# A three-block kernel: scale and shift applied to transposed rows at the start, a router in column quarters, and the state-space setup placed under a projection

## The reference, cut to what matters

```python
def first_block(x, c, ...):      # T = 256, D = 1024
    mod = silu(c) @ w_mod + b_mod                  # six vectors of 1024: sh1 sc1 g1 sh2 sc2 g2
    h = layer_norm(x) * (1 + sc1) + sh1            # "first modulation"
    ... = h @ w_in + b_in ...                      # ag, av, v, u, ga, gb
    x = post_norm(alpha * x + g1 * branch)
    h = layer_norm(x) * (1 + sc2) + sh2
    logits = h @ w_router + b_router               # 32 experts
    top 4 of 32 per row, softmax over the four     # "router"
    y = sum over the four of weight * expert(h)    # 32 experts, 12.6 MB of weights each
    return post_norm(alpha * x + g2 * y)
def second_block(...): ...                         # retention and a gated recurrence
def third_block(...):                              # GLA mixer, then an S5 mixer (state space)
    x = x + gla(...)                               # ends in a projection, "go"
    h = rmsnorm(x); u, z = split(h @ s5_w_in)
    # 64 groups x 64 complex states: lam_bar = exp(lam dt), rotate, scan in time, rotate back
    y = gelu(...); y = y * sigmoid(y @ w_glu + b) * silu(z); x = x + y @ w_out
    return rmsnorm(x)
```

## Time and profile before

| what | value |
|---|---|
| time, median of 3 runs | 2265.51 us |
| lowest and highest | 2263.78 and 2267.04 us |
| the profiled execution's own time | 2264.45 us |
| its span, first to last instruction | 2262.6 us |
| PE busy, share of the span | 2132.4 us, 94% |
| DVE, ACT, POOL busy | 782.6, 440.7, 73.0 us |
| mean granted TensorE clock | 0.988 |

### The profile page before, as it was taken

One profiled execution on the slowest core, in us unless ns is written; L12 is line 12 of the kernel. 1 busy time (PEld: TensorE's weight loads), 2 busy tenths in 40 slices (PEclk: granted clock), 3 DMA queues, 4 the chain that ended last, 5 costly groups with the idle time before them and its releaser, 6 DMA issues.

```text
span 2262.6 us, 30802 instructions
## 1 busy us (share of the span) xinstructions
PE 2132.4 (94%) x11644; PEld 1117.4 (49%) x11645; DVE 782.6 (35%) x1897; ACT 440.7 (19%) x886; POOL 73.0 (3%) x95
## 2 busy tenths in 40 slices
PE   6999999989999998999999998999999999998998
PEld 5745564333333333333333335745564446787873
DVE  1794443222222222222222222241212363998100
ACT  1011121101111110111101101031012215897100
POOL 0000000000000000000000000000000000222000
PEclk9999999999999999999999999999999999999999
DMA  9654677989989995998989999435234333232340
GB/s 374 222 187 153 243 281 279 418 337 418 411 351 418 417 417 232 418 416 333 418 344 418 418 418 369 159 126 186 75 126 149 112 119 114 76 113 75 124 159 34
DMA packets 157322, 591.38 MB, mean 261 GB/s; under 512 B 5073, under 2 KB 5137, under 8 KB 124353
## 3 DMA queue, kind: packets, MB, share of 16 engines
q1 hardware_dynamic: 152240, 572.03, 64.6%
q0 software_dynamic: 4384, 16.40, 2.0%
q10 hardware_dynamic: 624, 1.93, 0.2%
HBM read 589.29 MB, written 1.05 MB: 261 GB/s over the span
## 4 chain that ended last, share of the span: by engine, by line
PE 77%; ACT 8%; DMA 6%; DVE 4%; DVEq 2%; issue 1%; ACTq 1%; SPq 0%
PE PS L646 18%; PE PS L977 17%; PE PS L634 10%; PE PS L1000 9%; DMA W<-in_w_gu 5%; PE PS L675 4%; PE PS L661 4%; PE PS L1013 2%; PE PS L924 2%; ACT BIG L1609 1%; PE PS L1261 1%; PE PS L968 1%; DVE BIG L1973 1%; PE PS L941 1%; DVE BIG L1977 1%
## 5 line engine op out<-in xcount | busy, mean ns | idle before, releaser
L977 PE MATMUL PS<-W,BIG 128*64 128x512 f32 x2048 | 448.3, 594 | 6.3 <-DMA W<-in_w_gu 6.2
L646 PE MATMUL PS<-W,BIG 128*128 128x512 f32 x960 | 417.9, 596 | 4.3 <-DVE BIG L2443 2.9
L646 PEld LDWEIGHTS PS<-W,BIG 128*128 128x128 f32 x960 | 182.9, 191 | 231.6 <-issue 226.1
L977 PEld LDWEIGHTS PS<-W,BIG 128*64 128x64 f32 x2048 | 143.5, 137 | 293.3 <-issue 280.0
L1000 PE MATMUL PS<-W,BIG 128*64 128x512 f32 x1024 | 228.2, 598 | 6.9 <-ACT BIG L1423 6.9
L634 PE MATMUL PS<-BIG,W 128*128 128x256 f32 x1024 | 222.2, 379 | 1.5 <-ACT BIG L382 1.5
L634 PEld LDWEIGHTS PS<-BIG,W 128*128 128x128 f32 x1024 | 194.2, 190 | 29.0 <-ACT BIG L382 1.9
L1418 ACT ACTIVATE BIG<-BIG 128x512 f32<-128x512 f32 x32 | 20.2, 630 | 709.6 <-DVE BIG L1971 709.6
L1971 DVE TENSOR_SCALAR BIG<-PS 128x512 f32<-128x512 f32 (+1 forms) x38 | 24.7, 650 | 345.7 <-PE PS L977 321.6
L1000 PEld LDWEIGHTS PS<-W,BIG 128*64 128x64 f32 x1024 | 70.9, 137 | 143.3 <-issue 128.2
L1187 PE MATMUL PS<-BIG,W 128*128 128x256 f32 x512 | 118.7, 386 | 1.5 <-ACT BIG L1578 0.9
(11 more groups left out here) (482 smaller groups left out, 1978.5 us busy)
## 6 DMA issues: line engine op xcount, KB each, us to landing
W<-in_w_gu SPq DMA_DIRECT2D x128, 2048.0 KB, 14.7
W<-in_w_dn SPq DMA_DIRECT2D x64, 2048.0 KB, 15.2
W<-in_w_in SPq DMA_DIRECT2D x24, 2048.0 KB, 18.9
W<-in_w_mod SPq DMA_DIRECT2D x12, 2048.0 KB, 10.9
W<-in_gla_w_in SPq DMA_DIRECT2D x10, 2048.0 KB, 7.9
...
```

The source lines that it names most:

```text
L646: ins = pe.matmul(ps[:, t, :], lhs(i * KT + k)[:, t * P:(t + 1) * P], w[:, k, :], start=i + k == 0, stop=last_chunk and k == KT - 1)
L977: ins = pe.matmul(PS[hh[h], g, :], XET[:, k, :], gu_w(k)[:, g * D + h * CH:g * D + (h + 1) * CH], start=False, stop=k == KT - 1, skip_grou ...
```

## The change

It has three parts and some small ones.

**Head.** SP issues the first six chunks in the order 0, 2, 4, 5, 1, 3 (`HEAD_ORDER`). h1 is now only normed by DVE (one `tensor_scalar` for each row tile) and is transposed at once. `head_rows` makes the first half (512 columns) of sc1 and of sh1; ACT copies both; `head_columns` transposes them, so that each scale and shift value stands on the partition of its column; DVE multiplies and adds the transposed slices 0 to 3 in place. `head_unit` runs the part of ag0 and av0 that needs slices 0 to 3, then the second halves of sc1 and sh1 are made, then the rest of both units runs. No spread of sc1 and sh1 is left.

**Router.** The spread of sc2 stands ahead of the second half of sh2, the spread of sh2 directly behind it; of g2 only the first half is made ahead of the transposes. The logits are 16 matmuls with 128 x 32 weights and 128 columns, in four column quarters of the array (two slices summed in each), copied by DVE, and summed and transposed by two matmuls with `QUARTERS`. The second half of g2, three residual terms and the spread of g2 take the place of `keep_active`. ACT takes the exponentials ahead of the copies of g2, and makes the copies GAIN_Q and GAIN_H that DVE made. The product BDN goes to POOL. All bias sums stand directly ahead of the loop; PE waits for the table of extra blocks inside `extras`.

**State space.** `spread_b`, `rounded`, `turn_b`, `angles` and `trig` of groups 0 and 1 are done while PE runs go1 (with scratch of their own, `ANG` and `RND` in three places); the norm of the first row tile stands between them. u of group 0 is copied and stacked as soon as a quarter of the projection is done. `S5_EARLY` is 13, and in the last but one group the Gelu pass stands ahead of `y_out`.

```diff
-S5_CT, S5_P, S5_I, S5_G, S5_N, S5_EARLY = 16, 64, 16, 64, 128, 12
+S5_CT, S5_P, S5_I, S5_G, S5_N, S5_EARLY = 16, 64, 16, 64, 128, 13
+HEAD_ORDER = (0, 2, 4, 5, 1, 3)
...
+            for n in HEAD_ORDER:
+                mat, r, c = head_chunks[n]
+                sp.dma_start(slot(n), mats[mat][r:r + D, c:c + CH].rearrange("(k p) n -> p k n", p=P)) \
+                    .then_inc(w_landed[slot_no(n)], 16)
...
-                    pool.wait_ge(ev("mod_done"), len(MODS))
+                    pool.wait_ge(unit_free[UNIT["g2"][0] % 2], UNIT["g2"][0] // 2 + 1)
+                    pool.wait_ge(ev("moe_small_landed"), 80)
+                    pool.tensor_tensor(BDN, BDN, MA[0:NE], ALU.mult).then_inc(ev("exp_then_bias"), 1)
...
+                        if between and t + i == 1:
+                            between(t)
...
+            def head_rows(name, i):
+
+                j, at = MODS[name]
+                n = UNIT[name][3] + i
+                o = PS[:, 6 + j, i * P:(i + 1) * P]
...
+                pe.wait_ge(w_landed[slot_no(n)], load_count(n))
+                for k in range(KT):
+                    for q in range(4):
+                        ins = pe.matmul(o[32 * q:32 * q + 32, :], CB[:, k, :], slot(n)[:, k, q * P:(q + 1) * P],
+                                        start=False, stop=k == KT - 1, skip_group_check=True)
+                if name == "sh1":
+                    ins.then_inc(chunk_done, 3 if i else 1)
+
+            def head_columns(i):
+
+                pe.wait_ge(ev("mod_copied"), i + 1)
+                for j in range(2):
+                    ins = pe.transpose(HEAD_PS[:, j, :], MODROW[:, j, i * P:(i + 1) * P], ident)
+                ins.then_inc(ev("mod_done"), 1)
+
+            def head_unit(name, i, ms):
...
+                for m in ms:
+                    for k in range(4 * i, 4 * i + 4):
+                        if name == "ag0" and m == 0:
+                            pe.wait_ge(ev("cond_ready"), k + 2)
+                        ins = pe.matmul(ps[:, m // 2, (m % 2) * T:(m % 2 + 1) * T], slot(c0)[:, k, m * P:(m + 1) * P], hT[:, k, :],
+                                        start=k == 0 and m % 2 == 0, stop=k == KT - 1, skip_group_check=True)
...
+            head_rows("sc1", 0)
             for t in range(TT):
                 pe.wait_ge(ev("rows_ready"), NORMED["h1"] + t + 1)
                 row_to_columns("h1", t, h1[:, t])
...
+            head_rows("sh1", 0)
+            head_columns(0)
+            head_unit("ag0", 0, range(4))
+            head_unit("av0", 0, range(2))
+            head_rows("sc1", 1)
+            head_rows("sh1", 1)
+            head_unit("av0", 0, (2,))
+            head_columns(1)
+            head_unit("av0", 0, (3,))
+            head_unit("ag0", 1, range(4))
+            head_unit("av0", 1, range(4))
...
             mod_rows("sc2")
-            mod_rows("sh2")
+            mod_rows("sh2", (0,))
             mod_spread("sc2")
-            mod_rows("g2")
+            mod_rows("sh2", (1,))
             mod_spread("sh2")
-            mod_spread("g2")
+            mod_rows("g2", (0,))
...
             for t in range(TT):
-                for k in range(KT):
-                    ins = pe.matmul(PS[:, 6, t * NE:(t + 1) * NE], H2T[:, k, t * P:(t + 1) * P], WR[:, k, :],
-                                    start=k == 0, stop=k == KT - 1)
+                pe.wait_ge(tp_copied, TB["h2"] + 2 * t + 2)
+                for i in range(2):
+                    for q in range(4):
+                        k = 4 * i + q
+                        ins = pe.matmul(PS[32 * q:32 * q + 32, 6, t * P:(t + 1) * P], WR[:, k, :], H2T[:, k, t * P:(t + 1) * P],
+                                        start=i == 0, stop=i == 1, skip_group_check=True)
             ins.then_inc(ev("logits_done"), 1)
-
-            keep_active(4, 4)
-            pe.wait_ge(ev("neg_max"), 1)
-            keep_active(4, 2)
-            pe.wait_ge(ev("exp_ready"), 1)
-            keep_active(4, 5)
+            pe.wait_ge(ev("routed"), 1)
+            for t in range(TT):
+                ins = pe.matmul(PS[:, 6, T + t * NE:T + (t + 1) * NE], LOGITS_T[:, t * P:(t + 1) * P], QUARTERS,
+                                start=True, stop=True, skip_group_check=True)
+            ins.then_inc(ev("logits_done"), 1)
+            mod_rows("g2", (1,))
...
+            residual_in(0)
+            residual_in(1)
+            mod_spread("g2")
...
+            dense_by_rows("go1", lambda k: OGT[:, k, :], turn_b)
...
             fill_half(0, 0)
             fill_half(0, 1)
-            turn_b(1)
+            drive(0)
             fill_half(1, 0)
             within(0)
+            drive(1)
             fill_half(1, 1)
-            drive(0)
-            drive(1)
...
+            act.wait_ge(ev("routed"), 2)
+            for t in range(TT):
+                ins = act.activation(E4[:, t, :], V8[:, t, 0:4], ACT.Exp, bias=NM[:, t:t + 1], accum_out=ES[:, t:t + 1])
+            ins.then_inc(ev("exp_then_bias"), 1)
+            copy_mod("g2")
             wait_mod(act, "g2")
...
+            act.activation(mod_view(MA)[0:NE], gain[0:NE], ACT.Copy)
+            for q in range(4):
+                r = slice(XBLK * q, XBLK * (q + 1))
+                act.activation(GAIN_Q[r].rearrange("p (q c) -> p q c", q=2), gain[r, 2 * (q % 2):2 * (q % 2) + 2, q // 2], ACT.Copy)
+            for h in range(2):
+                r = slice(BLK * h, BLK * (h + 1))
+                ins = act.activation(GAIN_H[r].rearrange("p (q c) -> p q c", q=4), gain[r, :, h], ACT.Copy)
+            free_unit(ins, "g2")
             act.wait_ge(ev("pos_done"), 1)
...
             spread_b(0)
+            spread_b(1)
             rounded(0)
+            act_tile_rms(act, X, row(1), 0)
             turned_copy(0)
-            spread_b(1)
+            rounded(1)
+            trig(0)
+            turned_copy(1)
+            trig(1)
             spread_c(0)
...
+            stack_u(0)
             fill_copy(0)
...
             stack_u(1)
             for ct in range(S5_CT + 1):
-                if ct + 1 < S5_CT:
+                if 2 <= ct + 1 < S5_CT:
                     trig(ct + 1)
...
+                if ct == S5_CT - 2:
+                    act.wait_ge(ev("s5_out"), ct)
+                    spread_c(ct + 1)
+                    act.drain()
+                    act.activation(U16[:, 0:S5_EARLY, :], U16[:, 0:S5_EARLY, :], ACT.Gelu_apprx_tanh).then_inc(ev("s5_gelu"), 1)
...
+            norm_scale(dve, X)
+            for t in range(TT):
+                dve.tensor_scalar(h1[:, t], X[:, t], MV[:, t, 0:1], RS[:, t:t + 1], ALU.subtract, ALU.mult) \
+                    .then_inc(ev("rows_ready"), 1)
...
+            for i in range(2):
+                half_kt = slice(4 * i, 4 * i + 4)
+                dve.wait_ge(ev("mod_done"), i + 1)
+                dve.tensor_scalar_add(SCALE1[:, half_kt], HEAD_PS[:, 0, 0:P:32], 1.0)
+                dve.tensor_copy(SHIFT1[:, half_kt], HEAD_PS[:, 1, 0:P:32])
+                dve.drain()
+                for k in range(4 * i, 4 * i + 4):
+                    dve.tensor_scalar(hT[:, k, :], hT[:, k, :], SCALE1[:, k:k + 1], SHIFT1[:, k:k + 1], ALU.mult, ALU.add) \
+                        .then_inc(ev("cond_ready"), 1)
...
+            dve.wait_ge(ev("logits_done"), 1)
+            dve.tensor_copy(LOGITS_T, PS[:, 6, 0:T]).then_inc(ev("routed"), 1)
...
+            add_to_x("go", first_angles)
```

226 lines of the change are left out of this document (121 added, 105 removed).

## The result

The changed kernel takes 2254.44 us (median of 6 executions, 2241.50 to 2257.67) against 2266.28 for the kernel before: ratio 0.9945, 95% interval 0.9928 to 0.9963. That is faster, as forecast, but by 12 us where 21 were forecast, and outside the range of 2236 to 2252. The profiled execution happens to be the shortest: 2241.50 us (span 2239.7), less than the forecast of 2244. So two things need an explanation: the parts of the gain, and the 16 us between executions of one and the same kernel.

What follows compares the result with a forecast made beforehand. PE, busy for 94% of the span, was taken as the bound. Gains 6.5 + 6.3 + 6.0 + 2.3 = 21.1 us off the profiled 2264.45, with 1.06 added for the median, gave 2244; 8-in-10 range 2236 to 2252.

Steps and rivals of the forecast that it cites:

- Head, forecast 6.5: Head: ag0 and av0 end at 61.3 instead of 67.8, 6.5 us gained, from 5 to 8.
- State space, forecast 6.0 + 2.3: State space: start gains 6.0 us (4.5 to 8) by earlier sines of group 2; end 2.3 (1 to 3) by fewer table loads.
- The second sine table load: State-space start: ACT must load the sine table again before group 2's sines, 1.28 us, as the square root stood between.
- Router, forecast 6.3: Router: 6.3 us gained, taken in the middle between 9.6 at full clock and 2.7 at the low clock.
- Parts (a) to (c): Router: earlier spreads, transposes and shorter logits (2.1 to 3.1 us instead of 6.78) start DVE's choice 8.6 to 11 us earlier.
- Part (e): Router: ACT's g2 copies delay its copy of the weights: 0.9 us new wait at full clock, 4.9 at low.
- The small loads don't hold them: Router: the last small load, issued at 316.20, lands at 325.9, before the logits at 328.0, so costs nothing.
- BDN on POOL: Router: the product on POOL costs at most 3 us; bias sums come some ten us behind the g2 copies.
- at the low clock 8.1 - 4.9 - 0.5 = 2.7: Router's low-clock sum: 8.1 us earlier choice, less 4.9 new wait and 0.5 for turning rows, leaves 2.7 gained.
- Rival 1: Router: PE at low clock from transposes to gather, router gain 2.7 or less, time 2248; chance 0.25 of under 3.
- Rivals 2 and 3: Weight stream bounds the experts' loop, 2257, chance 0.08; ACT gives back the state-space start, 2252, chance 0.07.
- rival 4: State-space pipeline: DVE and POOL products collide, 18 us over 14 periods, or 31 and time 2275; chance 0.04.

Runs made afterwards that it cites:

- the mend of both: Router part alone on the kernel before, with BDN on DVE, eight bias-sum matmuls ahead of the first gather, eight ahead of the loop: mean 2257.6 us, ratio 0.9967.
- the mend on the whole change: Changed kernel with BDN on DVE, eight bias-sum matmuls ahead of the first gather and eight ahead of the loop: mean 2239.5 us, ratio 0.9885 against the kernel before.

## Why the prediction was right or wrong

**Head, forecast 6.5: right.** 6.6 us by the trace of the profiled execution; every moment named (27, 41.7, 61.3) came within 1.5 us. A part of its first half ran at 1.2 GHz (12.24 us instead of 10.4), and that was hidden by the wait for the sixth chunk.

**State space, forecast 6.0 + 2.3: right in mechanism, too small.** From xl0 to the last matmul 859.19 us became 847.38, that is 11.8. The step that the start rests on came as forecast: the sines of group 2 are 6.8 us earlier, and in the kernel before they run at the very start of its fall of the clock, so that these 6.8 us are a shorter wait and not clock. In the end part the table loads and what hangs on them gave 3.3 instead of 2.3. The start gave 5.7 up to the gate; 1.5 more came ahead of su0, where I had booked up to 0.9 as a cost: the wait of 1.73 us for the first spread b was on the path and went away. The rest, some 1.4 us, lies in the stage up to go1's end and the one behind the gate's start; the kernel before has a fall of the clock in each (at 1831 and at 2200) that the changed kernel's profile lacks. The second sine table load is there, as forecast.

**Router, forecast 6.3: wrong, and this is the step that failed.** Parts (a) to (c) were right, and near their upper end: logits 1.08 us, DVE's choice 10.8 us nearer (forecast 8.6 at the low clock, 11 at full clock). Part (e)'s new wait was right too (0.6 us, forecast 0.9). Three terms were not. First, "The small loads don't hold them": the last one landed 9.7 us behind its issue and held the logits for 1.62 us; this took nothing from the forecast figure, since the modulation ran at full clock. Second, "BDN on POOL" was priced by its own length and its deadline, not by what it does to DVE: 1.44 us on the path (6.44 less 5.00). I had the collision as a rival, but only in the pipeline, where it did not come. Third and largest, "at the low clock 8.1 - 4.9 - 0.5 = 2.7" was no lower bound. It charged the low clock only up to the choice and the copies of g2, and left the 8.75 us from gather to first expert, and the up projection behind them, as in the kernel before. The three profiles of the changed kernel show a low clock there: gather 1.7 us longer, the preparations 0.4 to 6, the first up projection 1.7 to 2.8. Alone, the part gave -0.1 us. What makes the clock fall there is shown only in part: pause and run of sixteen each go with it, and the mend of both helps, but the clock also fell without either (at 330.4 with the mend on the whole change).

**Range.** Rival 1 named the clock, but not the place: from the transposes to the pause it was 1.00 in the first profile and fell only at 332.7. Its price, a router part of 2.7 and 2248, was too low; with a router part of zero it would have given 2251. That is the mean of all 18 executions (2251.2), which lies inside the range, while the median of the first six (2254.44) does not. The upper end of 2252 was worked out with that same 2.7; with -0.1 in its place it would have been 2255. That the profiled execution took 2241.50, near the forecast, is luck: it is the shortest of the 18. The Trainium skill, TensorE: Matmul & The Clock Gate, section "HAM oscillation", which I weighed against the router part, says that idle gaps throw the array back to the slow clock, and it pointed the right way: in all five profiles with a pause of 3.7 us or more ahead of the gather the gather took 3.68 us instead of 1.94. The falls within the busy run are not what that section describes. Rivals 2 and 3 did not come, and for rival 4 the period is 10.77 us still (fill matmuls of su and sz at 1922.03, 1932.80, 1943.56).
